# Expert blocks in pairs, tokens behind half of the projection weights, 16-bit row tables

## The reference

```python
def expert_block(args):
    tok, e = args
    xb = xpad[tok]
    hb = jax.nn.silu(xb @ w_gate[e]) * (xb @ w_up[e])
    return hb @ w_down[e]
...
routed = jax.ops.segment_sum(rows.reshape(R, D) * row_gate[:, None].astype(xf.dtype), row_tok, num_segments=N + 1)[:N]
```

## Time and profile before

| | us |
|---|---|
| median of 3 runs | 1109.2 (1108.86 to 1109.27) |
| the profiled execution | 1107.19 |
| its span, first to last instruction | 1105.2 |

### The profile page before, as it was taken

How to read it: one execution, slowest core, us unless ns; L and a number is a source line. 1 busy time by engine, 2 the same in 40 slices (tenths; PEclk the granted TensorE clock), 3 DMA queues, 4 the chain that set the end, 5 groups by cost and what they waited for, 6 DMA issues and landing times.

```text
span 1105.2 us, 18276 instructions
## 1 busy us (share of the span) xinstructions
PE 1029.8 (93%) x7300; PEld 446.4 (40%) x7300; DVE 333.2 (30%) x816; ACT 225.9 (20%) x502; POOL 164.6 (15%) x238
## 2 busy tenths in 40 slices
PE   4899998988999999999999999999999999999385
PEld 0455556564454563333333333333333333333132
DVE  0212226764236763111111111111111111111177
ACT  1211106664123100111111111111111111111011
POOL 1000010300221110121221221221122122120000
PEclk9999999999999999999999999999999999999798
DMA  9954409201201606889999999999999999995595
GB/s 374 410 219 153 152 31 281 119 1 69 103 39 50 242 17 278 332 311 416 367 341 420 420 420 421 419 420 419 410 420 392 418 411 421 420 420 198 216 429 238
DMA packets 56620, 321.62 MB, mean 291 GB/s; under 512 B 10164, under 2 KB 10812, under 8 KB 27352
## 3 DMA queue, kind: packets, MB, share of 16 engines
q1 hardware_dynamic: 39056, 270.62, 60.9%
q0 software_dynamic: 14816, 43.34, 10.0%
q10 hardware_dynamic: 2664, 6.49, 1.5%
HBM read 299.86 MB, written 32.44 MB: 301 GB/s over the span
## 4 chain that ended last, share of the span: by engine, by line
PE 82%; DMA 11%; DVE 4%; ACT 1%; issue 1%; SPq 1%; POOLq 0%; DVEq 0%; ACTq 0%
PE bank L1828 29%; PE bank L1844 15%; PE bank L1451 8%; PE bank L1653 6%; DMA ring<-in_w_up 5%; PE bank L1807 4%; DMA ring<-expert_rows 4%; PE bank L1696 3%; DMA reg_p<-in_w_mod 2%; PE bank L1624 2%; PE bank L1702 2%; PE bank L1440 2%; PE bank L1709 2%; PE bank L1478 2%; PE bank L1610 1%; PE bank L1597 1%
## 5 line engine op out<-in xcount | busy, mean ns | idle before, releaser
L1828 PE MATMUL bank<-ring,reg_h 128*32 128x512 f32 x2672 | 354.1, 594 | 3.9 <-DMA ring<-in_w_up 1.7
L1828 PEld LDWEIGHTS bank<-ring,reg_h 128*32 128x32 f32 x2672 | 101.5, 110 | 204.2 <-issue 201.0
L1844 PE MATMUL bank<-ring,reg_y 128*32 128x512 f32 x1336 | 181.8, 595 | 1.1 <-ACT reg_y L917 1.1
L1340 DVE TENSOR_TENSOR reg_h<-reg_p,bank 128x256 f32<-128x256 f32 x51 | 21.5, 422 | 340.0 <-ACT reg_p L934 329.1
L1828 PE MATMUL bank<-reg_p,reg_h 128*32 128x512 f32 x592 | 121.4, 599 | 2.5 <-DMA ring<-in_w_up 2.5
L666 POOL DMA_INDIRECT expert_rows<-reg_y,rowc x51 | 51.4, 1009 | 443.5 <-DVE reg_y L1328 434.6
L934 ACT ACTIVATE reg_p<-bank 128x256 f32<-128x256 f32 x51 | 19.6, 384 | 331.3 <-PE bank L1828 331.3
L1451 PE MATMUL bank<-ring,reg_h 128*128 128x384 f32 (+2 forms) x256 | 84.4, 488 | 0.0
L1328 DVE TENSOR_SCALAR reg_y<-bank,reg_p 128x512 f32<-128x512 f32 x51 | 38.3, 751 | 140.4 <-PE bank L1844 140.4
L1844 PEld LDWEIGHTS bank<-ring,reg_y 128*32 128x32 f32 x1336 | 45.5, 109 | 81.6 <-issue 75.3
L1653 PE MATMUL bank<-ring,reg_h 128*128 128x512 f32 x160 | 70.1, 594 | 1.4 <-DVE reg_h L1141 1.4
(11 more groups left out here) (259 smaller groups left out, 936.6 us busy)
## 6 DMA issues: line engine op xcount, KB each, us to landing
ring<-in_w_gate SPq DMA_DIRECT2D x52, 1024.0 KB
ring<-in_w_up SPq DMA_DIRECT2D x52, 1024.0 KB
ring<-in_w_down SPq DMA_DIRECT2D x52, 1024.0 KB
ring<-in_w_mod SPq DMA_DIRECT2D x21, 1024.0 KB, 7.0
ring<-expert_rows SPq DMA_DIRECT2D x9, 2048.0 KB, 16.6
reg_p<-in_w_gate SPq DMA_DIRECT2D x12, 1024.0 KB
reg_p<-in_w_up SPq DMA_DIRECT2D x12, 1024.0 KB
reg_p<-in_w_down SPq DMA_DIRECT2D x12, 1024.0 KB
```

The lines of the kernel that those rows point to most:

```text
L1828: last = pe.matmul(bank[2 + p][R * j:R * j + R, :], xg_t[:, p, k * P + R * j:k * P + R * j + R], w_gu(homes[n % SLOTS])[:, k], start=(k == ...
L1844: last = pe.matmul(bank[5 + hf][R * j:R * j + R, :], h_t[:, p, i * P + R * j:i * P + R * j + R], w_dn(homes[n % SLOTS])[:, i, 512 * hf:512 ...
```

## The change

1. **Tokens.** The latent tokens are asked for on SP's queue, behind the second of four parts of w_in, and have a semaphore of their own. ScalarE does the squares and root of tile 0 as soon as the context tokens are there, and those of tiles 1 to 4 behind its half of h1 of tile 0; VectorE's reciprocal and scaling are split alike. TensorE's transposes of tile 1 move into the first projection, in front of k = 6.
2. **Row tables.** The one-hot matrices are bf16. bf16 holds the row number only in two parts, so `b_oh` holds two values per block, the row's multiple of 128 and the token's place (the partition), and the product has 214 columns. To make that possible the row number becomes `tile * 1024 + k * 128 + partition`. VectorE has one more operation per tile, and after the tables it adds the two parts and takes the token from the number by shifts and masks. The final reads view `expert_rows` in the new order, so what a partition reads for four choices is four rows of 4 KB, 512 KB apart, where it was one run of 16 KB.
3. **Expert loop.** TensorE's order per pair of blocks (b even) is: down b-2, gate/up b, down b-1, gate/up b+1, h of b, transposes of b+2 and b+3, h of b+1. The transposes of even blocks from 2 on go to banks 5 and 6 (down's banks), so down of an even block waits until they have been copied. The transposes of block 1 come before the loop, behind the last shared down product. ScalarE, VectorE and POOL follow the same order; POOL's gathers are issued two in a row, and a scatter no longer stands between.

```diff
@@ sync, start
+                if n == 1:
+                    sp.dma_start(xs[:, 1:T, :], x_sample[0].rearrange("(t p) d -> p t d", p=P)).then_inc(s_x, 16)
...
@@ sync, final reads
-                src = y_dram[t * P * TOPK:(t + 1) * P * TOPK, :].rearrange("(p k) d -> p k d", k=TOPK)
+                src = y_dram[t * P * TOPK:(t + 1) * P * TOPK, :].rearrange("(k p) d -> p k d", k=TOPK)
...
@@ gpsimd
+            next_gather(2)
+            next_gather(3)
+            for b in range(0, NQ, 2):
+                if b:
+                    next_scatter(b - 2)
+                    next_scatter(b - 1)
+                next_gather(b + 4)
+                next_gather(b + 5)
+            next_scatter(NQ - 1)
...
@@ scalar
             act.wait_ge(s_clr, 2)
+            act.wait_ge(s_xp, 16)
+            squares(0, 1, 1)
...
             h1_half(0)
+            act.wait_ge(s_x, 16)
+            squares(1, T, 2)
...
+            for b in range(0, NQ, 2):
                 if b:
+                    y_out(b - 2)
+                silu(b, 0)
+                if b:
+                    y_out(b - 1)
                 if b + 1 < NQ:
+                    silu(b + 1, 1)
+                h_t_out(b, 0)
+                for n in range(b + 2, min(b + 4, NQ)):
+                    xt_half(n, n % 2, bank[xt_banks(n)[0]])
+                if b + 1 < NQ:
+                    h_t_out(b + 1, 1)
+            y_out(NQ - 1)
...
@@ vector, tables
+                    link(dve.tensor_tensor(hit, iota[:, 0:NT].unsqueeze(1).to_broadcast([P, TOPK, NT]),
+                                           block_f[:, t, :].unsqueeze(2).to_broadcast([P, TOPK, NT]), ALU.is_equal))
+                    dve.tensor_tensor(blocks[:, :, 0, :], hit, row_f[:, t, :].unsqueeze(2).to_broadcast([P, TOPK, NT]), ALU.mult)
+                    dve.tensor_scalar(blocks[:, :, 1, :], hit, scal[:, 0:1], None, ALU.mult)
+                    dve.tensor_tensor(place, iota.unsqueeze(1).to_broadcast([P, TOPK, P]),
+                                      place_f[:, t, :].unsqueeze(2).to_broadcast([P, TOPK, P]), ALU.is_equal).then_inc(s_oh, 1)
...
-            link(dve.tensor_scalar(row_i[:], bank[6][:, 0:NT], float(NROW), None, ALU.add))
-            dve.tensor_single_scalar(tok_i[:], row_i[:], 3, ALU.logical_shift_right).then_inc(s_tab, 1)
+            link(dve.tensor_copy(row_p, bank[6][:, NT:2 * NT]))
+            link(dve.scalar_tensor_tensor(row_i[:], bank[6][:, 0:NT], float(NROW), row_p, ALU.add, ALU.add))
+            link(dve.tensor_scalar(tile_i, row_i[:], 10, 7, ALU.logical_shift_right, ALU.logical_shift_left))
+            link(dve.tensor_single_scalar(tok_i[:], row_i[:], P - 1, ALU.bitwise_and))
+            dve.tensor_tensor(tok_i[:], tok_i[:], tile_i, ALU.bitwise_or).then_inc(s_tab, 1)
...
@@ tensor
                 for k in range(KD):
+                    if k == KD - 2:
+                        xhat_t(1)
...
-                    last = pe.matmul(bank[6][:, 0:NT], a_oh[t % 2][:, k, :], b_oh[t % 2][:, k, :],
+                    last = pe.matmul(bank[6][:, 0:2 * NT], a_oh[t % 2][:, k, :], b_oh[t % 2][:, k].rearrange("p v b -> p (v b)"),
...
@@ tensor, block_down
+                if b % 2 == 0:
+
+                    pe.wait_ge(s_xa, min(b + 3, NQ))
+                    pe.wait_ge(s_xb, min(b + 3, NQ))
...
@@ tensor, expert loop
+            block_transposes(1, 1, 16)
             pe.wait_ge(s_shm, T)
+            for b in range(0, NQ, 2):
+                if b:
+                    block_down(b - 2)
                 block_gate_up(b)
                 if b:
+                    block_down(b - 1)
                 if b + 1 < NQ:
+                    block_gate_up(b + 1)
+                block_h(b, 0)
+                for n in range(b + 2, min(b + 4, NQ)):
+                    x_in(n)
+                if b + 1 < NQ:
+                    block_h(b + 1, 1)
             block_down(NQ - 1)
```

More of the change, by code:

```diff
@@ L202, in build, with halves @@
         h2t = view(reg_p, 0, KD, NTOK)
-        a_oh = [view(reg_h, 2176, TOPK, P), view(reg_h, 3200, TOPK, P)]
+        def halves(reg, off, n):
+            return reg[:, off:off + n // 2].bitcast(BF16)
+        a_oh = [halves(reg_h, 2176 + 512 * i, TOPK * P).rearrange("p (k q) -> p k q", k=TOPK) for i in range(2)]
         x2_tmp = view(reg_p, 5632, D)
@@ L677, in _, with next_gather, next_scatter @@
             gather(1)
[L679 to L686, removed]
[L687 to L689 removed]
+            copies = [2]
+            def next_gather(b):
+                if b < NQ:
+                    pool.wait_ge(s_xt, b - 1)
+                    pool.wait_ge(s_gc, b - 1)
+                    pool.tensor_copy(tokc[:, b % 2:b % 2 + 1], tok_i[:, b:b + 1]).then_inc(s_idx, 1)
+                    copies[0] += 1
+                    pool.wait_ge(s_idx, copies[0])
+                    gather(b % 2)
+            def next_scatter(b):
+                copies[0] += 1
+                scatter(b, b % 2, copies[0], 16 * (b // 2))
+            next_gather(2)
+            next_gather(3)
+            for b in range(0, NQ, 2):
+                if b:
+                    next_scatter(b - 2)
[3 more added lines that the diff above has]
+            next_scatter(NQ - 1)
             pool.wait_ge(s_trip, 1)
@@ L1039, in _ @@
             h1_half(0)
+            dve.wait_ge(s_std, 2)
+            link(dve.reciprocal(rstd[:, 1:T], rstd[:, 1:T]))
+            xhat(1)
             xhat(2)
@@ L1280, in _ @@
                     dve.wait_ge(s_tb, t - 1)
[L1281 to L1285, removed]
+                if t:
+                    dve.wait_ge(s_oh, t)
+                with nc.allow_low_precision("zeros, ones, tokens under 128 and multiples of 128 are exact"):
+                    link(dve.tensor_tensor(hit, iota[:, 0:NT].unsqueeze(1).to_broadcast([P, TOPK, NT]),
[4 more added lines that the diff above has]
+                                      place_f[:, t, :].unsqueeze(2).to_broadcast([P, TOPK, P]), ALU.is_equal).then_inc(s_oh, 1)
             link(dve.tensor_scalar(x_cmp, xinc, scal[:, 4:5], None, ALU.is_le))
@@ L1800, in _, with block_transposes @@
               .then_inc(s_erow, 1)
-            def block_transposes(b, p, gathered):
+            def block_transposes(b, p, gathered, banks=(0, 1)):
                 pe.wait_ge(s_xg[p], gathered)
@@ L1806, in block_transposes, with x_in @@
                 for k in range(KD):
-                    last = pe.transpose(bank[k // 4][:, (k % 4) * P:(k % 4 + 1) * P], v[:, k, :], ident)
+                    last = pe.transpose(bank[banks[k // 4]][:, (k % 4) * P:(k % 4 + 1) * P], v[:, k, :], ident)
                 last.then_inc(s_xt, 1)
+            def x_in(b):
+                if xt_banks(b)[0] == 5:
+                    at_least(pe, s_ya, b - 2)
+                    at_least(pe, s_yb, b - 2)
+                block_transposes(b, b % 2, 16 * (b // 2 + 1), xt_banks(b))
             def block_h(cb, p):
```

110 lines of the change are left out of this document (53 added, 57 removed).

## The result

The changed kernel takes 1096.97 us (median of 4 runs, 1095.87 to 1099.83) against 1109.03 for the kernel before in the same session: ratio 0.990, 95% interval 0.9883 to 0.9916. That is 12.1 us faster by the medians, 9.3 to 13.0 by the interval. Between the two profiled executions the step is smaller, 1107.2 to 1097.6 (span 1105.2 to 1095.8): -9.6.

What follows compares the result with a forecast made beforehand. The prediction took the expert loop as paced by the weights' landing from 560 us on, with TensorE almost as fast. Terms -4.4 - 0.7 - 5.3 + 3.0 = -7.4 gave 1101.8 us for the median, range 1093 to 1107.5.

Steps and rivals of the forecast that it cites:

- Start: Up to the first projection's end: tokens behind half of w_in let the projection start and end earlier, -4.4 us.
- rival B: Front gives only 2 us (late w_in or lower-clock first projection), row tables cost 1.3: 1106.2 us; chance 0.13.
- Row tables: Table stage: 16-bit products take 0.9 us, VectorE replaces TensorE as what is late, -0.7 us.
- Expert loop: Loop in pairs of blocks: only 3.6 us before DMA is full and 1.7 at the end are gained, -5.3 us.
- The mechanism of the landing: In the expert loop, weights' landing is fixed once DMA is full; only requests early by then gain, 3.6 us.
- Rival A: The expert loop follows TensorE after all and gives 16.7 us: 1090.4 us; chance 0.13.
- Final reads: Reads at the end: 4 KB pieces instead of 16 KB runs read more slowly, fully exposed, +3.0 us.
- Rival C: Final reads fall to half the rate as pieces lie 512 KB apart, 43.7 us more: 1142.5 us; chance 0.07.
- From the execution to the median: Whole kernel: the sum gave 1099.8 us for the profiled execution, 2.0 under its median, so 1101.8 for the median.

Runs made afterwards that it cites:

- x9_again: The changed kernel itself, unaltered, run once more: 1094.87 us, ratio 0.9874 to the kernel before.
- x10_contiguous: The changed kernel with the old row order (16 KB runs in the final reads) kept beside 16-bit tables: 1092.99 us, ratio 0.9855 to the kernel before.
- light old loop: The kernel before with half of each w_down left out of the loads from the sixth expert on: 1103.81 us, ratio 0.9954.

## Why the prediction was right, and where its sizes were off

*Start: -4.4 forecast, -4.2 in the pair of traces, -4.5 by the run of this part alone.* Right in sum, with two errors inside that cancel, which is luck. Forecast were the last piece at 27.4, the projection from 32.7 and its end at 55.1; it was 25.74, 31.91 and 55.4. The 0.6 us wait for the third part of w_in did not come in this trace (in x9_again and x10_contiguous it did, with 0.4 and 0.7 us). The first 48 products took 17.44 us where 15.6 are due at 2.6 us per k: the granted clock was partly at the lower level, 0.79 over 32 to 40 us and 0.68 over the stretch before it, where the kernel before had 1.00 from 8 to 56 us. This is one half of rival B, a first projection that starts at the lower clock, and four of the five traces with the new front show it (granted 0.79 to 0.83 over 32 to 40 us). Waits included, these products take 16.4 to 18.4 us in the five, against 15.6 to 17.3 in the nine with the old front; the earlier start paid for it. The two stretches of the changed kernel:

```profile
24.00:32.00 8.00, 5.37 (x29) 2.28 (x21) 2.44 (x9) 1.51 (x4) 0.00 (x0) 0.68 1.01 416
32.00:40.00 8.00, 8.00 (x20) 4.58 (x21) 0.00 (x0) 0.37 (x1) 0.00 (x0) 0.79 1.02 412
```

Over all traces the gain is larger. QK starts at 182.1 to 185.2 with the old front (nine traces, mean 183.5) and at 177.5 to 178.7 with the new one (five, mean 178.0): 5.6 us. The trace of before that I worked from was one of the quick ones, 1.2 us under that mean.

*Row tables: -0.7 forecast, -2.1 measured.* The mechanism was right (VectorE replaces TensorE as what is late, table products of 0.9 us), the size of one term was not: 0.65 us for the new TENSOR_SCALAR, taken from the f32 rows, is 0.44. The Trainium skill ("VectorE: DVE Perf Modes", the tier table) had the better figure. By it I had worked out 0.37 and -2.2, and the trace agrees nearly: 0.44 and -2.1. The trace also agrees with its condition ("What auto-detection actually checks", that every tensor be 16-bit) on the operation next to it: a TENSOR_TENSOR with one f32 operand got nothing from its other operand's 16 bits (1.05 us before and after).

*Expert loop: -5.3 forecast, -7.0 in the pair, -8.1 by the part alone.* TensorE's own part, 10.8 forecast, is 10.0: 1.0 at the head where I had 2.1, 23 x 0.33 in the pairs where I had 24 x 0.29, and 1.4 at the end (block 48 to the end is 39.84 us in the light old loop, 38.43 in the paired) where I had 1.7. The term that was mis-sized is what is left of that: I let the loop gain only the lead of the weights' landing at the time when DMA fills up, 3.6 us, and 1.7 at the end. Over the traces with normal bytes the old loop takes 606.4 to 610.3 us (five, mean 608.4), the paired one 599.6 to 601.3 (five, mean 600.1): 8.3 apart, where I had 5.3.

The mechanism of the landing held, at nearly its size. Counted from the loop's start, SP's queue has its last 150 MB of weights still to bring at 141.0 us in the old order and at 136.8 in the paired one (means of five), and from there until 3 MB are left it stays 3.6 to 4.9 us ahead, 4.2 on average: a lead that is built up early and then neither grows nor shrinks. The date was off: in steps of 50 us the old loop moves 337, 382, 361, 407 and then 421 GB/s (means of five), so DMA is full from some 200 us on and not from the 137 that I took from a stretch beginning at 590. The 2.2 MB that all queues together are ahead after 200 us would be 5.3 us at 417 GB/s, but a third of them are gathers and scatters asked for earlier, which bring no weight.

What failed is the step from this lead to TensorE, "a quicker TensorE there mostly buys longer waits". TensorE's waits for weights were 3.7 to 4.4 us in the five old loops (mean 4.1) and 4.3 to 7.2 in the paired ones (mean 5.4), so only 1.3 us went into longer waits, and the 7.2 of the changed kernel's trace, inside the forecast's 5 to 12, is the largest of the five. Of TensorE's own 10.0 us the loop keeps 8.3. Block 48 starts 567.5 us into the old loop and 561.6 into the paired one (means of five), 5.9 earlier, and behind it come 2.4 more. In the old order it was held by its weights in all five traces, for 1.7 to 2.6 us, with a low-clock group behind that in three; in the paired order the wait is at most 0.24 us, and no low-clock group follows. Of the 2.4 us, 1.4 are TensorE's own and 1.0 is the mean share of those groups, to which the forecast gave nothing. Of the 5.9 us, 4.2 are the weights' lead; for the other 1.7 I have no run, and they stay open.

Rival A (the loop follows TensorE, 16.7 us, the waits gone) is out as it was priced: the waits did not go, and its price is twice what the loop gave. But 8.3 of 10.0 lies nearer to a loop that follows TensorE than to my 5.3 of 10.8; only with more bytes (6.3) does the landing take a large part.

*Final reads: +3.0 forecast, +2.1 in the pair, +2.3 over 14 traces.* The reads ran at 411 GB/s, at the upper edge of the forecast's 380 to 410; its price came from the rate of the last four short reads (378), and long reads in 4 KB pieces do better than those. Rival C is out. The Trainium skill ("DMA: Bandwidth & Descriptors", Latency and other measured facts) gives 207 GB/s for rows 512 KiB apart from partition to partition, but 214 as the full rate of such a copy, so it tells of almost no loss at this step; I had put it beside rival C as if it told of a large one. With the step inside a partition's pieces no loss by the distance is to be seen here either: the tail is as long with the pieces 8 KB apart.

*What no part of the sum had: +1.7 between the shared experts' gate/up and the first table.* Twelve products of one line, in the changed kernel's first trace and in that of x9_again:

```profile
349.47 7.07 PE L1747 MATMUL bank<-ring,reg_p 128*128 128x512 f32 x12
```
```profile
348.83 5.37 PE L1747 MATMUL bank<-ring,reg_p 128*128 128x512 f32 x12
```

1.7 us more for the same work: part of it ran at the lower level of the clock (granted 0.76 from 349.47 to 356.50, against 1.00 from 348.83 to 354.20 in x9_again). The code is the same in all 14 kernels there, and the stage takes 37.7 us in five traces and 39.4 in nine.

*From the execution to the median.* I set the profiled run 2.0 us under the median and carried that over. The changed kernel's profiled run lay 0.6 above its median instead. So -9.6 between the traces and -12.1 between the medians are no contradiction: the trace of before has the quick front (1.2 us) and not that low-clock stretch (1.7 us), that of after has the stretch. These two fit the difference; no run shows that they are its cause. The means of the stages over all traces give -5.6 for the start, -2.1 for the tables, -8.3 for the loop and +2.3 for the tail, -13.7 together, near x9_again's -14.0: over all traces the forecast's -7.4 was further off than the first result says.

## What to carry to other kernels

When two resources are nearly level, don't take the slower one's progress as the whole loop's. Ask from which microsecond on, counted from the loop's start, the second one is full, and how far ahead the quicker order's weights are by then, in their own queue: bytes of all queues together would have given 5.3 us here where the weights had 4.2. Then count which waits the lead removes, with the low-clock groups behind them: in the old loops a group cost 1.7 us behind waits of 2.1 to 2.6. Price a 16-bit VectorE operation by its operands, not by the nearest f32 row. And split an index so that the layout of the large transfers stays long and contiguous (a multiple of 256 and a remainder under 256 fit 16-bit tables as well as any other split): the layout was the only part of this change that cost time.

## What the runs showed of the hardware that was not expected

A low-clock stretch of TensorE can be a matter of the single execution, and at 1.7 us it is as large as the terms under study: the stage before the tables has one in nine of 14 traces without a difference in its code, and of the changed kernel's two traces one has it. In the loop such a stretch followed some waits for weights and not others: the changed kernel's wait of 3.79 us at 778.52 had none behind it, that of 2.89 us at 944.07 had one (8.63 instead of 7.05 us). The other four paired loops have nearly the same wait, 3.75 to 3.81 us, before the same block, and all four have a low-clock group behind it (8.77 to 9.76 us).
